# Feed-forward second products: sums of squares, job foldings and coefficients placed behind the next weight split, job transposes moved into the next unit

## The reference

```python
def _swiglu(h, wg, wu, wd):
    return (jax.nn.silu(h @ wg) * (h @ wu)) @ wd        # wg, wu: 1024 x 2816, wd: 2816 x 1024
def _ada(c, w, b):
    mod = jax.nn.silu(c) @ w + b                         # w: 1024 x 9216 for each layer
    return mod.reshape(c.shape[0], N_SUB, 3, c.shape[-1])
def _sub_in(x, mod, i, g_pre):
    return _rmsnorm(x, g_pre) * (1.0 + mod[:, i, 1][:, None]) + mod[:, i, 0][:, None]
def _sub_out(x, mod, i, g_post, out, res_w):
    return x + res_w * (1.0 + mod[:, i, 2][:, None]) * _rmsnorm(out, g_post)
```

## Time and profile before

| | us |
|---|---|
| median of 3 runs | 2310.9 (2310.68 to 2312.05) |
| the profiled execution's own time | 2309.9 |
| its span | 2308.1 |
| PE busy in the span | 2257.8 (98%) |
| DVE busy | 1603.1 (69%) |
| ACT busy | 950.5 (41%) |
| POOL busy | 297.2 (13%) |

### The profile page before, as it was taken

How to read it: one execution, slowest core, us unless ns; L and a number is a source line. 1 busy time by engine, 2 the same in 40 slices (tenths; PEclk the granted TensorE clock), 3 DMA queues, 4 the chain that set the end, 5 groups by cost and what they waited for, 6 DMA issues and landing times.

```text
span 2308.1 us, 45009 instructions
## 1 busy us (share of the span) xinstructions
PE 2257.8 (98%) x18506; PEld 2166.1 (94%) x18506; DVE 1603.1 (69%) x2863; ACT 950.5 (41%) x1985; POOL 297.2 (13%) x362
## 2 busy tenths in 40 slices
PE   8999999999998999999999999999999999999999
PEld 6999999988887999999999999998888889999999
DVE  5588858676677756667675887666777777888523
ACT  4222223355566422223342222334555564455533
POOL 0000003221113300001230000033211142000000
PEclk9999999999999999999999999999999999999999
DMA  8356546432223145444524555442433321334322
GB/s 276 117 169 177 170 124 170 111 92 84 84 82 100 38 126 151 144 144 146 150 75 128 174 165 154 149 130 77 119 113 113 104 74 47 92 93 110 93 76 73
DMA packets 392796, 277.63 MB, mean 120 GB/s; under 512 B 11136, under 2 KB 349856, under 8 KB 392592
## 3 DMA queue, kind: packets, MB, share of 16 engines
q1 hardware_dynamic: 385792, 254.77, 37.9%
q0 software_dynamic: 6800, 19.99, 2.7%
HBM read 263.48 MB, written 12.81 MB: 120 GB/s over the span
## 4 chain that ended last, share of the span: by engine, by line
PE 86%; DVE 9%; issue 2%; ACT 2%; DMA 1%; SPq 0%; POOL 0%; DVEq 0%; ACTq 0%; POOLq 0%
PE lin L1242 56%; PE lin L1603 10%; PE lin L1438 6%; PE lin L1262 2%; PE ps_o L1748 2%; PE ps_s L1661 2%; DVE acc L2940 1%; PE ps_s L1438 1%; DMA raw<-in_ffn_w_down 1%; DVE w_lo L2818 1%; DVE h_lo L3057 1%; PE ps_s L1318 1%; DVE x L3031 1%; DVE sums L2992 1%; PE lin L1222 1%
## 5 line engine op out<-in xcount | busy, mean ns | idle before, releaser
L2818 DVE TENSOR_TENSOR w_lo<-raw,w_hi 128x1024 fp32r<-128x1024 f32 (+1 forms) x272 | 331.0, 1220 | 190.2 <-ACT w_hi L2069 189.2
L1242 PE MATMUL lin<-h_hi,w_hi 128*128 128x272 f32 x2096 | 453.8, 290 | 2.1 <-DVE w_lo L2818 1.9
L1242 PE MATMUL lin<-h_hi,w_lo 128*128 128x272 f32 x2096 | 451.1, 289 | 0.0
L1242 PE MATMUL lin<-h_lo,w_hi 128*128 128x272 f32 x2096 | 449.8, 288 | 0.0
L2069 ACT ACTIVATE w_hi<-raw 128x1024 fp32r<-128x1024 f32 (+1 forms) x272 | 280.1, 1038 | 197.5 <-DMA raw<-in_ffn_w_down 144.3
L1242 PEld LDWEIGHTS lin<-h_hi,w_hi 128*128 128x128 f32 x2096 | 336.0, 188 | 3.6 <-issue 2.7
L1242 PEld LDWEIGHTS lin<-h_lo,w_hi 128*128 128x128 f32 x2096 | 336.6, 189 | 0.0
L1242 PEld LDWEIGHTS lin<-h_hi,w_lo 128*128 128x128 f32 x2096 | 334.6, 189 | 0.0
L2940 DVE SCALAR_TENSOR_TENSOR acc<-raw,silu_c,acc 128x512 f32<-128x512 f32 x448 | 313.9, 761 | 0.0
L1242 PE MATMUL lin<-act_hi,w_hi 128*128 128x272 f32 x1280 | 280.6, 289 | 5.4 <-DVE w_lo L2818 5.2
L1242 PE MATMUL lin<-act_hi,w_lo 128*128 128x272 f32 x1280 | 277.8, 288 | 0.0
(11 more groups left out here) (468 smaller groups left out, 4355.8 us busy)
## 6 DMA issues: line engine op xcount, KB each, us to landing
raw<-in_w_ada SPq DMA_DIRECT2D x128, 512.0 KB, 3.9
raw<-in_ffn_w_gate SPq DMA_DIRECT2D x88, 512.0 KB, 4.1
raw<-in_ffn_w_up SPq DMA_DIRECT2D x88, 512.0 KB, 3.9
raw<-in_ffn_w_down SPq DMA_DIRECT2D x64, 448.0 KB, 3.8
raw<-in_ffn_w_down SPq DMA_DIRECT2D x32, 512.0 KB, 4.5
raw<-in_w_in_ab SPq DMA_DIRECT2D x24, 512.0 KB, 4.8
raw<-in_w_in_c SPq DMA_DIRECT2D x24, 512.0 KB, 3.8
start_w<-in_w_ada SPq DMA_DIRECT2D x16, 512.0 KB, 11.8
```

Source lines behind the costliest of these rows:

```text
L1242: m = nc.tensor.matmul(out[a], w_tile(w, k), mv[:, k0 + k, half(a)], start=first and k == 0 and n == 0, stop=last and k == u["tiles"] - 1 ...
L2818: nc.vector.tensor_tensor(w_all(w_l, u["tiles"]), src, w_all(w_h, u["tiles"]).bitcast(F32), ALU.subtract).then_inc(lo_done, 1)
```

## The change

In DVE's loop over the units of the second product, at the place i: `fold` of a job whose last piece was unit i - 1, and the squares of a block whose last chunk was unit i - 1, now stand after `split` of unit i + 1 and ahead of `accumulate` of unit i. Before, the fold stood right behind the fourth `accumulate`, and the squares stood in the loop of their own unit, behind its `accumulate` and ahead of the next `split` (only where a fold stood there too were they already held until after it). `coefs` moves from the end of place first + 5 to the place between the squares and `accumulate` of place first + 6. On PE `turn_job` moves from behind unit first + 4 into unit first + 5, ahead of its third tile.

```diff
@@ PE, project
-                sums_behind = {f + 4: n for f, n in DN_JOBS[j].items()} if kind == "ffn" else {}
+                sums_in = {f + 5: n for f, n in DN_JOBS[j].items()} if kind == "ffn" else {}
...
+                        if part == 0 and i in sums_in:
+                            mid = {2: lambda n=sums_in[i]: turn_job(n, j)}
...
-                        if part == 0 and i in sums_behind:
-                            turn_job(sums_behind[i], j)
@@ DVE, accumulate
-            def accumulate(n, k):
+            def accumulate(n, k, folds=True):
...
-                if k == JOB_U - 1:
+                if k == JOB_U - 1 and folds:
                     fold(nth)
@@ DVE, project_ffn
+                    if i - JOB_U in DN_JOBS[j]:
+                        fold(JOB_POS[DN_JOBS[j][i - JOB_U]] - len(START))
                     if held is not None:
                         add_squares(j, held, 0)
                         add_squares(j, held, 1)
                         held = None
+                    if i - 6 in DN_JOBS[j]:
+                        coefs(DN_JOBS[j][i - 6])
                     p = piece_at(DN_JOBS[j], i)
                     if p is not None:
-                        accumulate(*p)
+                        accumulate(*p, False)
                     if c == 2 and 0 < m < 6:
-                        if p is not None and p[1] == JOB_U - 1:
-                            held = m
-                            continue
-                        add_squares(j, m, 0)
-                        add_squares(j, m, 1)
-                    if i - 5 in DN_JOBS[j]:
-                        coefs(DN_JOBS[j][i - 5])
+                        held = m
```

## The result

| | before | after |
|---|---|---|
| median, us | 2310.79 (2310.52 to 2312.05, 6 runs) | 2318.27 (2315.65 to 2321.15, 6 runs) |
| ratio, 95% interval | | 1.0032 [1.0023, 1.0042] |
| profiled execution, us | 2309.9 | 2317.97 |
| its span, us | 2308.1 | 2316.1 |

What follows compares the result with a forecast made beforehand. The prediction took PE, busy 98% of the span, as the bound, so only its waits counted. Terms of 3.4 (j = 0), 0.6 (j = 2) and 0.6 (j = 3) gave +4.6 on 2310.9: 2315.5 us, range 2309.0 to 2319.5.

Steps and rivals of the forecast that it cites:

- 8.1 us rule: Second products: the end of an accumulation plus 8.1 us is the earliest start of the unit three further on.
- (a): j = 0: transposes 1.5 us later delay the next job's first piece and unit 7's weights; unit 7 waits 0.7 us.
- (b): j = 0: squares and coefficients delay unit 6's accumulation 2.7 us; unit 8 waits 0.6, unit 9 1.9, job 13's transposes 0.45.
- (c): j = 0, units 10 to 16: further waits of 0.1 to 1.9 us; j = 0 loses 8.2 instead of 4.8, +3.4 us.
- (d): j = 2 and j = 3: (a) costs nothing; by (b) unit 9 waits 1.9 us, unit 8 0.4; +0.6 us each.
- (e): j = 5: no pieces and idle DVE, so moved squares cost and win nothing.
- Faster: Rival, chance 0.12: late splits in j = 0, 2 and 3 worth 4.7 us all go, giving 2306.2 us.
- The rule of the Trainium skill: DVE instructions with two SBUF operands and GpSimd ones exclude each other; by it alone the change would win, size not given.
- No net change: Rival, chance 0.15: late loads cost as much as the early splits win, within 2.5 us.
- worse: Rival, chance 0.05: delays of (b) add up from pair to pair, about +9 us in j = 0, 2322 in all.

Runs made afterwards that it cites:

- turn_only: Kernel before with only PE's transposes moved into the next unit; folds, squares and coefficients as before: 2316.19 us, ratio 1.0021.
- acc_first: Changed kernel with the accumulation put ahead of squares and coefficients, still behind the split: 2310.75 us, ratio 0.9999 of before.
- squares_only: Kernel before with only the squares moved, behind the next split and ahead of the accumulation: 2309.99 us, ratio 0.9997.
- squares_behind_acc: Kernel before with only the squares moved, behind the next split and also behind the accumulation: 2306.70 us, ratio 0.9979.
- combined: Kernel before with squares behind the accumulation everywhere, folds and transposes moved as in the change only in j = 2 and 3: 2305.44 us, ratio 0.9977.
- coefs_behind: Changed kernel with only the coefficients put back behind the accumulation: 2314.02 us, one run.

## Why the prediction was right, and where it was off

The forecast was slower, 2315.5 us within 2309.0 to 2319.5. The median is 2318.27 (2317.21 in the repeat): the side was right, the range held, the size was 1.5 to 3 us short.

**The 8.1 us rule** held. From the end of unit 6's accumulation to the start of unit 9 in j = 0 it is 8.2 us in the changed kernel, and in turn_only, with another order, 8.4 (357.62 to 366.01). The accumulation itself ended 2.6 us later than before (359.36 less 1.58, for 355.21), where 2.7 were forecast. The weights landed 5.3 us after their issue, as the rows of before said (5.4). That the late accumulation is the cause, and not just a neighbour of it, is shown by acc_first and by the pair squares_only and squares_behind_acc: moving only the accumulation ahead of the moved work is worth 2.75 to 3.2 us in j = 0 in the one, and 3.4 us (+0.23 to -3.18) in the other.

**(a)** held: the first piece started at 344.42, less the 1.6 us by which this stage began late 342.8, the time that was forecast, and unit 7 waited 0.58 for 0.7. What I did not see is how much this step weighs alone. I let the moves on DVE and on PE add up to one delay; turn_only shows 4.89 us from the transposes by themselves, of which DVE's new order gives some back. That the sum of j = 0 came out is in part luck: two parts of other sizes than I thought, which offset each other. "(a) costs nothing" in j = 2 and j = 3 isn't borne out for the transposes alone either (+0.50 and +0.76, near the spread of a stage, with unit 10's wait up from 0.70 to 1.08), though together with the moved folds they win there.

**(b) and (c)** held in sum: 8.1 us of waits (8.5 in the second trace) for the forecast 8.2. Unit 8 waited 0.62 for 0.6, unit 9 1.86 for 1.9, the transposes of job 13 0.84 for 0.45, unit 15 1.73 for 1.9, unit 16 0.29 for 0.3. Unit 11 was overrated (0.99 for 1.7), units 10 and 13 didn't wait (0.1 and 0.3 forecast); unit 14 waited more (0.51 for 0.3), and 0.19 and 0.50 us stand where none was forecast. These misses cancel, so the sum is better than its terms. So j = 0 lost 3.34 us, 3.83 in the second trace, for +3.4.

**(d)** was mis-sized in j = 2: 1.26 and 1.34 us for +0.6. Its own sum, 2.3 for 1.6, is +0.7, and with the 1.95 us of waits that j = 3 had before, +0.35 there. Unit 9 waited 2.18 for 1.9 and unit 8 0.75 for 0.4. The trace shows the squares behind the split, where they meet POOL's last operation for this block (1080.74 to 1082.35), and the accumulation behind them:

```profile
1081.64 2.12 DVE L2992 TENSOR_TENSOR sums<-sums,work 128x544 f32<-128x544 f32 x2
...
1084.88 2.74 DVE L2940 SCALAR_TENSOR_TENSOR acc<-raw,silu_c,acc 128x512 f32<-128x512 f32 x4
```

The two take 2.12 us where 1.54 is their time alone, 0.6 us more for the 0.4 in the forecast. Less the 4.89 us by which this stage begins later (1043.35 for 1038.46), the accumulation starts at 1080.0 for the forecast 1079.8. The load of unit 9, issued at 1088.06, landed at 1093.70, 5.6 us later and not 5.4. In j = 3 the waits rose by 0.4 to 0.6 us against the first trace of before, but the second trace of before waited 2.65 us there, more than the changed kernel in either trace (2.58 and 2.38). So a loss in j = 3 from the waits is not shown.

**(e)** held: +0.01 us in j = 5.

**The term that was missing** is the clock. The waits of this change add up to 5.2 to 5.6 us (3.34 or 3.83, 1.3, 0.4 to 0.6), and the medians differ by 6.2 to 7.5. (Ahead of the prediction it says that the clock was at full speed in every slice; the page gives one rounded digit for each 58 us and hides short stretches.) The rest of j = 3's +2.17 us in the first trace lies right behind the wait of 2.02 us at unit 9. Its windows there:

```profile
1504.00:1508.00 4.00, 2.17 (x18) 1.98 (x17) 1.88 (x3) 2.97 (x8) 0.70 (x1) 1.00 0.77 248
1508.00:1512.00 4.00, 4.00 (x22) 4.00 (x22) 4.00 (x5) 1.59 (x4) 3.84 (x4) 0.60 0.01 2
```

and the same unit in the second trace of the same code:

```profile
1504.00:1508.00 4.00, 2.37 (x19) 2.18 (x19) 2.89 (x3) 3.98 (x10) 1.64 (x2) 1.00 0.58 197
1508.00:1512.00 4.00, 4.00 (x34) 4.00 (x33) 4.00 (x4) 0.58 (x1) 2.52 (x3) 1.00 0.01 2
```

After the wait PE worked without a pause in both, but got through 22 matmuls at a granted clock of 0.60 in the one and 34 at 1.00 in the other. That costs some 1.6 us. The forecast kept the waits under 2 us and priced a wait at its length; a wait of about 2 us can cost another 1.6 us behind it, not each time. The gap between 5.4 and 6.2 to 7.5 us goes with the clock of the timed executions: the 16 of the changed kernel have a mean granted clock of 0.9964, the 55 of before that the experiments are compared with (without the one of 7955 us) one of 0.9974. Among those at 0.997 the changed kernel took 2316.5 us in the mean (6 executions) and before 2311.1 (14): 5.4 us, what the waits add up to. At 0.995 they took 2320.4 (4) and 2314.4 (3).

Where in the timed executions these stretches lie isn't known. Behind a wait of this change the traces show one only, the one above. The second trace of the changed kernel has none in the second products; its stretches lie at about 476, 1612, 1856 and 1984 us, in passages that the change doesn't touch, and the two traces of before have theirs at about 44, 1608 and 1848 and at 44, 472 and 1844 us. So a part of the 1 to 2 us can be chance, or a shift in time of the same work, and not the waits.

**The rivals.** "Faster" named a real sum: late splits of 4.7 us, and combined is 5.3 us faster than before. But it isn't won by work put ahead of the accumulation: that order gives +0.23 us in j = 0 where the other gives -3.18. The rule of the Trainium skill that stood beside it (SBUF — State Buffer, Who interferes with whom) agrees with the traces in single rows, and DVE's busy time did fall by 6.6 us. But not where I had looked: in the view that groups DVE's instructions by line the splits into `w_lo` fell from 331.0 to 328.2 us, those into `l_slot` from 10.9 to 8.7, accumulations and folds by 1.5 and 1.2, while the squares themselves rose from 55.7 to

```profile
L2992 DVE TENSOR_TENSOR sums<-sums,work 128x544 f32<-128x544 f32 (+1 forms) x68 | 59.1, 869 | 14.6 <-ACT work L2103 10.0 <-ACT work L2099 2.4
```

(busy us, mean ns, idle time before them and who ended it). Before, DVE waited 100.3 us for ACT ahead of the squares and 190.2 us ahead of the splits; now 14.6 and 251.6. DVE's idle time went from one place to another, and time that DVE saves there is worth nothing as long as the load behind its accumulation is late. "No net change" and "worse" are both ruled out by the intervals and by j = 0's +3.3 to +3.8.

## What to carry to other kernels

When an in-order engine serves two customers, here a split for PE and an accumulation that frees a buffer for a load 8 us ahead, work that nobody waits for goes behind both: the same squares gave a time of 0.9997 of before between the two and 0.9979 behind them. Before moving a producer later "into cover", look for the consumer on another engine that already waits for it: two tiles of delay of four transposes cost 4.9 us in j = 0, since the next job's first step hung on them. Don't judge such a change by the busy time of the engine that was rearranged; read the waits of the engine that bounds the kernel, and count waits of 2 us as possibly more than their length.

## What the runs showed of the hardware that was not expected

- Waits of about 2 us on PE can be followed by a stretch at the half clock level (1.2 instead of 2.4 GHz). Of four equal waits of 2.38 us three were, at 1.6 us each. Of the waits between 1.8 and 2.3 us in the two traces of the changed kernel, one was (2.02 us) and others weren't (1.86 and 2.18 in the first trace, 1.82, 1.94, 2.10 and 2.24 in the second); in coefs_behind one of 2.08 us was. The Trainium skill (TensorE: Matmul & The Clock Gate, HAM oscillation — how this bites in real kernels) describes this for a kernel that waits some 3 to 5 us for its loads between blocks of matmuls, with the clock falling each time; here the traces show it for shorter waits, and for some of them only. What decides between them stays open.
- The landing of the same kind of load, the weights of unit 9 issued 0.42 us behind a piece, took 5.1 to 5.7 us in j = 0 over the twelve traces, 5.3 to 5.9 in j = 2 and 5.1 to 6.9 in j = 3. The 6.9 are combined's (issued at 1485.52, landed at 1492.42) and leave its wait of 1.52 us in j = 3. The kernel before had 6.0 and 6.6 there in its two traces, so much of it differs between executions of the same code; why j = 3 differs most isn't settled.
- The same two squares on DVE took 1.54 us with POOL idle, 2.12 beside one of its operations (after, j = 2) and 2.50 beside several (turn_only, j = 0).
